# Unread matmuls during the routing, three and a half expert chunks asked for early, and the two experts of a pair run one behind the other

## The reference, cut to what matters

```
def hier_moe(h, w_rg, b_rg, w_re, b_re, w_eg, w_eu, w_ed):   # 256 tokens x 1024
    lg = t @ w_rg + b_rg                     # 4 groups; the best one is taken
    le = einsum('nd,dge->nge', t, w_re) + b_re   # 8 experts in each; the best two of the group
    gates = ...                              # 256 x 32, two nonzero values in each row
    for e in range(N_EXPERTS):               # 32
        hid = silu(t @ w_eg[e]) * (t @ w_eu[e])      # 1024 x 512 each
        out = out + gates[:, e:e + 1] * (hid @ w_ed[e])   # 512 x 1024
```

## Time and profile before

| what | value |
|---|---|
| time before, median of 3 runs | 1775.36 us (1773.78 to 1776.03) |
| the profiled execution, its time | 1774.61 us |
| the profiled execution, its span | 1772.8 us |
| TensorE busy | 1685.0 us, 95% of the span |
| first matmul of the experts' gather | 162.4 us |
| first turn's gate 0 starts | 169.15 us |
| last product of the experts' scatter starts | 628.5 us |

### The profile page before, as it was taken

One profiled execution on the slowest core, in us unless ns is written; L12 is line 12 of the kernel. 1 busy time (PEld: TensorE's weight loads), 2 busy tenths in 40 slices (PEclk: granted clock), 3 DMA queues, 4 the chain that ended last, 5 costly groups with the idle time before them and its releaser, 6 DMA issues.

```text
span 1772.8 us, 25754 instructions
## 1 busy us (share of the span) xinstructions
PE 1685.0 (95%) x10708; PEld 1308.8 (74%) x10708; DVE 894.3 (50%) x1502; ACT 752.4 (42%) x1154; POOL 111.8 (6%) x117
## 2 busy tenths in 40 slices
PE   7998989889998989999999999999999999999998
PEld 6976334433443369888899988888888889988886
DVE  6584211121112065644478977536654457987743
ACT  4563011111111145645556455424665545645532
POOL 0000000000000001400200000000240110000000
PEclk9998999999999999999999999999999999999999
DMA  7444999999999946323333454535423333354552
GB/s 285 164 155 190 421 427 429 428 429 428 427 430 428 425 181 238 125 114 143 143 143 143 170 207 186 204 145 230 192 103 143 143 143 144 143 190 184 188 206 84
DMA packets 31813, 412.15 MB, mean 232 GB/s; under 512 B 3648, under 2 KB 5216, under 8 KB 6496
## 3 DMA queue, kind: packets, MB, share of 16 engines
q1 hardware_dynamic: 31712, 410.70, 58.0%
HBM read 408.85 MB, written 1.84 MB: 232 GB/s over the span
## 4 chain that ended last, share of the span: by engine, by line
PE 83%; DMA 9%; DVE 3%; ACT 2%; issue 1%; SPq 0%; POOL 0%; POOLq 0%; DVEq 0%; ACTq 0%
PE bank L1145 9%; PE bank L1294 8%; PE bank L1299 8%; PE bank L1295 8%; DMA work_mem<-in_w 7%; PE bank L1713 7%; PE bank L1330 4%; PE bank L1329 4%; PE bank L1328 4%; PE bank L1717 3%; PE bank L1168 3%; DMA wring<-in_w 2%; PE bank L1354 2%; PE bank L1355 2%; PE bank L1360 2%
## 5 line engine op out<-in xcount | busy, mean ns | idle before, releaser
L1997 ACT ACTIVATE w_hi<-wring 128x2048 fp32r<-128x2048 f32 x84 | 161.1, 1918 | 222.8 <-PE bank L1329 101.3
L2763 DVE TENSOR_TENSOR w_lo<-wring,w_hi 128x2048 fp32r<-128x2048 f32 x84 | 192.2, 2292 | 121.7 <-ACT w_hi L1997 121.7
L1997 ACT ACTIVATE w_hi_early<-wring 128x2048 fp32r<-128x2048 f32 x84 | 160.7, 1914 | 201.3 <-PE bank L1295 136.7
L1294 PE MATMUL bank<-mixed,w_hi_early 128*128 128x256 f32 x928 | 232.3, 288 | 3.5 <-DVE w_lo L2763 3.5
L1295 PE MATMUL bank<-mixed,w_hi_early 128*128 128x256 f32 x928 | 227.3, 283 | 0.0
L2763 DVE TENSOR_TENSOR w_lo<-wring,w_hi_early 128x2048 fp32r<-128x2048 f32 x84 | 191.7, 2286 | 44.5 <-ACT w_hi_early L1997 44.1
L1294 PEld LDWEIGHTS bank<-mixed,w_hi_early 128*128 128x128 f32 x928 | 177.5, 191 | 8.4 <-DVE w_lo L2763 4.1
L1145 PE MATMUL bank<-wring,gates_mem 128*64 128x512 f32 x768 | 171.7, 604 | 11.4 <-DMA wring<-in_w 11.4
L1295 PEld LDWEIGHTS bank<-mixed,w_hi_early 128*128 128x128 f32 x928 | 177.8, 192 | 0.1
L2665 DVE TENSOR_TENSOR gates_mem<-bank,gates_mem 128x512 f32<-128x512 f32 x32 | 22.1, 692 | 251.0 <-ACT gates_mem L1945 140.6
L1145 PEld LDWEIGHTS bank<-wring,gates_mem 128*64 128x64 f32 x768 | 57.8, 139 | 113.2 <-issue 113.1
(11 more groups left out here) (504 smaller groups left out, 3072.7 us busy)
## 6 DMA issues: line engine op xcount, KB each, us to landing
wring<-in_w SPq DMA_DIRECT2D x160, 2048.0 KB, 8.6
work_mem<-in_w SPq DMA_DIRECT2D x32, 2048.0 KB, 18.1
cst<-in_const SPq DMA_DIRECT2D x1, 1224.0 KB, 15.9
prm<-in_prm SPq DMA_DIRECT2D x3, 381.0 KB, 7.9
x_mem<-in_x SPq DMA_DIRECT2D x2, 512.0 KB, 4.5
out_x<-x_mem SPq DMA_DIRECT2D x2, 512.0 KB, 2.6
rel_skew<-work_mem SPq DMA_DIRECT2D x1, 768.0 KB, 3.5
work_mem<-in_prm SPq DMA_DIRECT2D x1, 512.0 KB, 16.7
```

The lines of the kernel that those rows point to most:

```text
L1294: pe.matmul(out, w[0][:, k, cols], x[0][:, k, :], start=(k == 0), stop=False)
L1997: act.activation(hi, w, ACT.Copy).then_inc(hi_ready, 1)
L2763: dve.tensor_tensor(lo, w, hi, ALU.subtract).then_inc(lo_ready, 1)
```

## The change

In the first block, on TensorE: `keep_clock` issues matmuls of 512 columns whose result nobody reads, 3 ahead of each router product and 12 after the second one. The rank matmuls use the one-pass type. `member` is now made directly from the picked experts, and the gate values are worked out later (`gate_values`), behind the first `one_hot`. The second copy of the second transposed tile moves from VectorE to ScalarE. `xn_lo` of the second tile is made in two halves.

The transfers: chunk 0 and chunk 2 are asked for where 2 and 4 were, and right behind them chunk 6 and half of chunk 3, into memory that is free by then. Chunks 1, the other half of 3, 4 and 5 follow after the output projection, chunk 7 in two halves as soon as `member` is ready. `gain_row` goes behind the last expert chunk. In the first turn a chunk is asked for when the first expert's half of a job has ended.

In `hidden` and `down` the loop over the two experts goes outside: all matmuls of the first expert, then all of the second, and each waits for its own chunk alone.

In the stick-breaking step the two float32 matmuls of a head become four one-pass ones, on a high and a low part of the softplus values. GpSimd makes the parts, with a copy and a subtraction of 128x768 for each pair of heads.

```diff
-        for c, j in ((2, pre["vd"][1]), (4, pre["pv"][1]), (0, pre["out"][3]), (1, pre["out"][3]), (3, pre["out"][3]),
-                     (5, pre["out"][3])):
+        ahead_chunk(0, pre["vd"][1])
+        ahead_chunk(2, pre["pv"][1])
+        sp.dma_start(ahead_six, expert_source(6, 0)).then_inc(x_loaded[0], 16)
+        sp.dma_start(ahead_slot(3)[:, cols], expert_source(3, 0)[:, cols]).then_inc(x_loaded[0], 16)
+        ahead_chunk(1, pre["out"][3])
+        ahead_chunk(3, pre["out"][3], slice(0, CHUNK_COLS // 2))
+        ahead_chunk(4, pre["out"][3])
+        ahead_chunk(5, pre["out"][3])
+        sp.wait_ge(member_ready, TT)
+        for n, half in enumerate(ahead_seven):
+            sp.dma_start(half, expert_source(7, 0)[:, cols]).then_inc(x_loaded[1], 16)
+        for g in range(AHEAD_CHUNKS, AHEAD_CHUNKS + MOE_SLOTS):
+            c = g - AHEAD_CHUNKS
+            if c % 2:
+                sp.wait_ge(bank_full[j.bank], j.count(0))
+            else:
+                sp.wait_ge(first_half_used, 16 + c // 2 + 1)
+            expert_chunk(g % turn_chunks, g // turn_chunks)
...
+        def keep_clock(j, times):
+            free(j)
+            for _ in range(times):
+                pe.matmul(psum[j.bank][:, :], yo_hi[:, 0, 0:P], yo_hi[:, 0:2, :], start=True, stop=True)
         for i, j in enumerate(pre["router"]):
             turn_tile(i, TT + i + 1, ...)
+            keep_clock(j, 3)
             in_sbuf(pre["h2"][2 * i:2 * i + 2])
...
-        pe.wait_ge(member_ready, 1)
         j = pre["rank"][0]
+        keep_clock(j, 12)
+        pe.wait_ge(member_ready, TT)
...
-                for k in range(KT):
-                    for e in range(2):
-                        mm = pe.matmul(psum[j.bank][half, :], x_e[:, k, pair, half], w[e][:, k, :], ...)
+                for e in range(2):
+                    half, w = slice(e * CAP, (e + 1) * CAP), hidden_weight(name, pair, e)
+                    for k in range(KT):
+                        mm = pe.matmul(psum[j.bank][half, :], x_e[:, k, pair, half], w[k], ...)
...
-                    pe.matmul(b[:, 0:384], C("sufneg"), sp_, ...)
-                    pe.matmul(b[:, P:S], negtriu[:, P:S], sp_[:, S:384], ...)
+                    for part in (sp_hi, sp_lo):
+                        pe.matmul(b[:, 0:384], sufneg_r, part[:, n + r, :], ...)
+                    for part in (sp_hi, sp_lo):
+                        pe.matmul(b[:, P:S], minus, part[:, n + r, S:384], ...)
...
+            for n in range(0, SB_N, 2):
+                pool.wait_ge(sb_ready, 8 * l + n + 2)
+                pool.tensor_copy(flat(sp_hi[:, two, :]), flat(p_s[:, two, :])).then_inc(pool_step, 1)
+                pool.tensor_tensor(flat(sp_lo[:, two, :]), ..., ALU.subtract).then_inc(pool_step, 1)
```

More of the change, by code:

```diff
@@ L466, in program @@
     slot_gate = stat(PAIRS)
[L467 removed]
+    gain_row = view(pt_mem, 2048, D)
     at2 = {n: prm2[:, s] for n, s in PRM2.items()}
@@ L704, in _, with ahead_chunk @@
+        def ahead_chunk(c, j, cols=slice(0, CHUNK_COLS)):
             sp.wait_ge(bank_full[j.bank], j.count())
[L705 to L715, removed]
+            sp.dma_start(ahead_slot(c)[:, cols], expert_source(c, 0)[:, cols]).then_inc(
+                first_pass.w_landed[(c + AHEAD_CHUNKS) % MOE_SLOTS], 16)
@@ L727, in _ @@
                 expert_chunk(c, last_turn)
+        sp.dma_start(gain_row, d["gain"][0]).then_inc(gain_loaded, 16)
         sp.wait_ge(crowded_ready, 1)
@@ L1138, in hidden @@
                 ready(j)
[L1139 to L1146 removed]
+                for e in range(2):
+                    half, w = slice(e * CAP, (e + 1) * CAP), hidden_weight(name, pair, e)
+                    for k in range(KT):
+                        if (name, pair, e) == ("gate", 0, 0) and k % 2 == 0:
+                            copied(r["pick", 0][k // 2])
+                        mm = pe.matmul(psum[j.bank][half, :], x_e[:, k, pair, half], w[k], start=(k == 0), stop=(k == KT - 1))
+                    if e == 0 and r is first_pass and isinstance(turn, int) and turn == 0:
+                        mm.then_inc(first_half_used, 1)
                 mm.then_inc(r.bank_full[j.bank], 1)
@@ L1163, in down @@
                 ready(j)
[L1164 to L1169, removed]
+                for e in range(2):
+                    w = weight("down", pair, e).rearrange("p (k n) -> p k n", k=4)[:, :, n * 512:(n + 1) * 512]
+                    half = slice(e * CAP, (e + 1) * CAP)
+                    for ft in range(4):
+                        mm = pe.matmul(psum[j.bank][half, :], hid_t[:, pair, ft, half], w[:, ft, :], start=(ft == 0), stop=(ft == 3))
                 mm.then_inc(r.bank_full[j.bank], 1)
@@ L2591, in _, with xn_low @@
+        def xn_low(half):
+            cols = slice(half * 512, (half + 1) * 512)
+            dve.tensor_tensor(xn_lo[:, 1, cols], xn[:, 1, cols], xn_hi[:, 1, cols], ALU.subtract).then_inc(xn_lo_ready, 1)
         dve.wait_ge(a_ready, DA_HEADS)
```

149 lines of the change are left out of this document (109 added, 40 removed).

## The result

The changed kernel takes 1873.38 us (median of 4 runs, 1872.65 to 1874.13); the kernel before takes 1775.69 us (1773.78 to 1776.13) beside it. The ratio is 1.0552, 95% interval 1.0537 to 1.0566: slower by 5.5%, 98 us, where I had forecast 1760 us.

A forecast was written before the change was run, and what follows sets the result against it. The expert phase was taken to be bound by its chunk transfers, the later layers by TensorE. 1774.6 - 10.6 (expert phase) - 4.8 (stick-breaking) = 1759.2, forecast as 1760 us; own range 1752 to 1769, wider range 1751 to 1785.

The forecast's parts named there:

- The order of the two experts: In `hidden` and `down`, TensorE passes a 16-record run to the other half, at 1.0 us extra a turn.
- My second rival: Expert jobs: only a run's last four records overlap; turn 65.9, time about 1865; chance 0.09 together with large start cost.
- a large start cost: Expert turns: the second half starts late enough to make the kernel slower, 1778 to 1870; 0.09 together with passed-in-part.
- from 2.1 us extra a turn: Expert turns: the extra TensorE time at which it reaches the transfers' rate and the 15 us are used up.
- the 15 us of gains: Whole kernel: the forecast savings, 10.6 us in the expert phase and 4.8 us in stick-breaking.
- my first rival: Expert jobs: the second expert starts only when the first is done; +36 us a turn, about 2000 us; chance 0.10.
- The stream: Expert chunk transfers: more chunks early and an earlier gate 0 end them at 608.4 instead of 619.0, gaining 10.6 us.
- The routing: Before the experts: `pick` starts at 158.8 instead of 162.4, gate 0 at 164.0 instead of 169.15.
- (a): Routing: three unread matmuls keep full clock, so the second `turn_tile` ends at 150.7 instead of 152.4.
- (e): Routing: `pick` at full clock takes 3.8 us and `turn_hot` 1.3, so gate 0 starts at 164.0.
- Stick-breaking: Later layers: a head takes 0.69 instead of 0.99 us, 4.8 us less for 16 heads (bounds 1.9 and 6.7).

The follow-up runs named there:

- the alternating version: Changed kernel with only the expert order undone: halves alternate from matmul to matmul in `hidden` and `down`, jobs wait for both chunks; 1766.57 us, ratio 0.9946.
- With the branch moved: The alternating version with TensorE's branch on `crowded` moved from the first turn to the same place in the second; 1765.85 us, ratio 0.9945.
- without the unread matmuls too: The alternating version with the branch on `crowded` moved to the second turn and the `keep_clock` matmuls removed; 1763.36 us, ratio 0.9936.
- the kernel before with the branch moved: The kernel before the change, with only TensorE's branch on `crowded` moved from the first turn to the second; 1777.59 us, ratio 1.0013.
- the one with runs of 8: Changed kernel with gate and up in runs of four matmuls, 8 records, alternating between the two experts; 1776.70 us, ratio 1.0007.

## Why the prediction was wrong, point by point

**The order of the two experts: this step failed, and it set the sign.** I took it that "the run is passed as well, since two heads' runs in a row behave so". The rows behind it show a run of four records passed, and four is exactly how far TensorE reaches: one under way and three unstarted. Everything that I read from those rows was right; carrying it from 4 to 16 was not, and the text itself said that no row shows a run so long. With 0.43 us a record, a turn's 192 half-array records are 82.6 us one after the other; at the 13 changes of run that have no other work in between, four records overlap and save 1.72 us each, 22.4; the 10.4 us of gather, transpositions and scatter come on top: 70.6, measured 71.3. My second rival had this mechanism ("if only the last four records of a run overlap with the next"), and shared a chance of 0.09 with a large start cost. That its 1865 came within 8 us is luck, by two errors against each other. Its turn of 65.9 us was 5.3 too short: the `down` jobs were left as they were, and a hidden job was put at 10.3 us, where the three in a row take 33.04 / 3 = 11.0. And it charged most of the 13.8 us by which TensorE is busier, although 6.6 of them fit under the transfers. Eight turns of 65.9 instead of 58.7 would have given some 1825. The same slip stands in "from 2.1 us extra a turn": from 52.1 to 58.8 are 6.7 us before anything is lost, and with the 15 us of gains it takes 8.6.

The rule of the Trainium skill that I weighed, that matmuls start and end in program order ("TensorE: Matmul & The Clock Gate", Part 3), would have given some 2000 us by my first rival. The runs don't agree with it: three records are passed by those of the other half. Its sign was right all the same: slower.

**The stream: right in its form, one term left out.** I wrote that "chunks 8 to 17 last until 222.1". Chunk 14 can't be asked for before `down` of pair 0 has freed the slot of chunk 8, and ahead of that lies TensorE's pause at its branch. In the alternating version, between the landings of chunks 13 and 15 lie some 16 us instead of 9.8. That gap of some 6 us is the size of what the stream ended too late by, 5.7 us (614.1 against the 608.4 of my sum). With the branch moved it ended at 610.2, and without the unread matmuls too at 607.6. So the branch as the cause of the gap is shown, in one profiled execution of each; that the time follows it is shown for these executions and not for the medians, which differ by 0.7 us.

**The routing.** Gather at 158.8, as forecast; gate 0 at 165.48 for 164.0, because `pick` ran mostly at 1.2 GHz. The gain of the unread matmuls, my steps (a) and (e), fell: the clock of the second `turn_tile` can be 1.00 without them and that of `pick` is low with them. What is left of the 3.7 us that the stretch from the second `turn_tile` to gate 0 lost belongs in the main to the shorter chain to `member`: with the second `turn_tile` at full clock and no unread matmuls it took 19.8 us with the old routing (the kernel before with the branch moved) and 17.3 and 16.7 with the new one.

**Stick-breaking.** 0.70 us a head, as forecast, 4.8 us in all; 2.6 to 3.1 arrive in the later layers. One part of the difference shows: behind the second pair of heads TensorE now waits for `w_lo`, twice 0.5 us.

```profile
908.87 0.33 PE L1641 MATMUL bank<-exact 128*128 128x256 f32 x1
909.69 0.50 PE L1427 MATMUL bank<-w_hi_early,mixed 128*128 128x512 f32 x1 [0.48 <-DVE w_lo L2872]
```

```profile
907.49 2.82 POOL L2358 CAST sp_hi<-work_mem 128x768 fp32r<-128x768 f32 x1 [10.09 <-DVE work_mem L3067]
```

VectorE makes the first `w_lo` from 907.35, right behind the softplus, in 2.28 us beside GpSimd's copy; before it took 2.29 (from 805.49), and TensorE read at 807.83. So VectorE isn't slowed there: the start of L1427 hangs on its chain, and what the heads save ahead of it can't arrive. The second `w_lo`, beside GpSimd's subtraction, takes 2.91 us instead of 2.29. GpSimd itself was hidden, though the copy took 2.8 us and the subtraction 3.77 in the median (1.85 at the least) for the 1.8 that I had put for each. That GpSimd's and VectorE's subtractions slow each other (3.77 for 1.85, 2.91 for 2.29) agrees with the Trainium skill, "GPSIMD Engine Reference", 1. Specifications, which has GpSimd share its memory interface with VectorE's instructions of two inputs.

## What to carry to other kernels

When two matmuls share the array by halves, alternate them in the program, or keep the runs short: here runs of two records (one float32 matmul) lost nothing, and four ran beside the next four in rows 7; eight kept the later turns at 58.7 us but ended each job of the first turn some 1.7 us later, sixteen cost a fifth of the turn. A reordering that an engine does by itself has a reach; before you lean on it, count how long the run is in the row that shows it, and if yours is longer, treat it as the likely loss. A stream through a ring of slots is to be followed slot by slot until it is steady: what frees each slot, and which pause of the reader lies ahead of that.

## What the runs showed of the hardware

Three unstarted float32 matmul records of one half of the columns are passed by those of the other half, and no more, whether a record has 512 or 256 columns, and with or without a semaphore wait between the runs.

A branch on TensorE left a standstill of 3.0 to 4.9 us between the last record ahead of it and the first behind it (start to start) in the alternating versions and the one with runs of 8, where the chunks had landed and records have 512 columns, and none in the changed kernel, where the halves run one behind the other. In four of the five profiles of such a standstill the granted clock was 0.50 for a few microseconds behind it (pairs of records at 0.85 us instead of 0.43).
